# The last FFN pair multiplied with tokens on partitions, fused with the transposes of the final norm

## The chip, the cores and the metric

The kernel runs on one core of one Trainium2 chip. The metric is the device time of one execution in microseconds (us). Engines are called by the profile's names: PE (TensorE matmul), PEld (its weight load), DVE (VectorE), ACT (ScalarE), POOL (GpSimd) and SP (SyncE, which here only issues DMAs).

## The reference, cut to what matters

One layer of a streaming encoder over 1024 prompt and 64 sample tokens, with 1024 features. What counts here is its end: the second half-step feed-forward network (FFN, 2816 hidden features) and the final RMSNorm.

```python
def _rmsnorm(x, g):
    y = x * lax.rsqrt(jnp.mean(x * x, axis=-1, keepdims=True) + EPS)
    return y * g

def _swiglu_half(x, g, w_gate, w_up, w_down):
    h = _rmsnorm(x, g)
    return 0.5 * ((jax.nn.silu(h @ w_gate) * (h @ w_up)) @ w_down)

x = x + _swiglu_half(x, g_ffn2, w2_gate, w2_up, w2_down)    # (1088, 1024)
y = _rmsnorm(x, g_final)                                    # the first two outputs
```

## The kernel before, in words

All 1088 tokens (T) stay on the chip as X, features on partitions: eight tiles (KT) of 128 features by 1088 tokens. The tokens are cut into three tiles NTILE of 364, 362 and 362. Each engine has its own instruction stream, written out by hand; the streams meet in semaphores only, and each executes its instructions in the order of the code.

The down projection of an FFN runs over 11 pairs of 128-feature groups of the hidden layer (p = 0 to 10, LAST = 10). For each pair, SP loads the two activation tiles (AR) and the two weight tiles (RAWD). ACT rounds them to fp32r as the high parts (`down_high`, L1144 and L1147), POOL and DVE subtract to get the low parts (`down_a_low`, L1159, and `down_low`, L1154). Buffers alternate: AB and WB of index 2 (ABe, WBe in the trace) hold the even pairs and so the last one. PE then runs `pe_down`: for each of 3 token tiles and 8 feature tiles a chain of six matmuls (two groups, each as hi·hi, hi·lo and lo·hi in `three_pass`, L248 to L250), with the weights stationary and 362 or 364 tokens moving, into one of six banks in turn (DOWN_BANK). DVE adds half of each chain's result to X (`dve_x`, L1194). That is 24 chains and 24 adds for a pair.

After the last pair PE waits for all adds, and transposes X to tokens on partitions, in nine blocks of 128 tokens (the last has 64): two banks of 512 features for each, four transposes to a bank (L2468), with four blocks of banks in turn. For each block ACT squares and sums each bank (L1850), DVE adds the two sums (L2174), ACT takes the root (L1852), DVE the reciprocal (L2176), and DVE multiplies by it and by the gain GF while it copies the two banks to YO (L2182). SP stores the block (L1401, and L1403 for the sample block). PE takes block b's banks again when YO of block b-4 is written. POOL loads GF, the gain broadcast to all partitions, behind the last chain of the last pair (L1600), because GF lies on the bytes of WBe; DVE waits for that load before its first step of the norm.

Of the kernel before, what the change touches and what calls it, by code (L numbers as in the profile page):

```python
# [13 lines left out]
F32 = mybir.dt.float32  # L14
F32R = mybir.dt.float32r
ACT = mybir.ActivationFunctionType
ALU = mybir.AluOpType
AX = mybir.AxisListType

P = 128  # L20
D = 1024
KT = D // P
SEQ, DEC = 1024, 64
T = SEQ + DEC
NB = SEQ // P
# [30 lines left out]
def build(nc, a, o):  # L56

    with ExitStack() as ctx:
# [4 lines left out]
        def place(name, shape, dtype, offset):  # L63
            return nc.alloc_sbuf_tensor_at(name, shape, dtype, offset=base + offset)
# [14 lines left out]
        rWG = region("wg", 2 * 4 * 4096)  # L79
        rRAW = region("raw", 4 * 4096)  # L80
        rD = region("d", 3 * 8192)
# [4 lines left out]
        X = place("X", [P, KT, T], F32, rX)  # L86
# [27 lines left out]
        AB = [place("AB0", [P, 2, 2, T], F32R, rHL), place("ABo", [P, 2, 2, T], F32R, rHL + 4 * T * 4), place("ABe", [P, 2, 2, T], F32R, rA)]  # L114
        WB = [place("WB0", [P, 2, 2, D], F32R, rWG), place("WBo", [P, 2, 2, D], F32R, rWG + 16384), place("WBe", [P, 2, 2, D], F32R, rD)]
        AR0 = place("AR0", [P, 2, T], F32, rD + 26112)
        AR = [[place(f"AR{f}{i}", [P, 2, T], F32, (rX, rHH)[f] + (2 - i) % 2 * 2 * T * 4) for i in range(2)] for f in range(2)]
        RAWD = [place("RAWDe", [P, 2, D], F32, rRAW), place("RAWDo", [P, 2, D], F32, rRAW + 8192)]
# [38 lines left out]
        assert 4096 + LH * (LD + 4) * 4 <= 7552 and 9600 + 2048 <= 8 * NW * 4  # L157

        YO = place("YO", [P, 4, D], F32, rHH)
        GF = place("GF", [P, D], F32, rD)  # L160
        JUNK = place("JUNK", [P, 4, 512], F32, rT)


# [54 lines left out]
        def named(prefix, names):  # L218
            return namedtuple(prefix, names)(*[sem(f"{prefix}_{n}") for n in names.split()])
# [16 lines left out]
        mo_in = sem("mo_in")  # L236
        m_ = named("m", "d qw ex kt vt gt kw v ot s asm num cn w dn sq norm v2 rs rc sc yt y hi lo cs cout")
        att_hi, att_lo, o_add = sem("att_hi"), sem("att_lo"), sem("o_add")
        fin = named("fin", "sum y")
        fin_out = [sem(f"fin_out{i}") for i in range(4)]  # L240

        def x_view(k, n):
# [883 lines left out]
                    pe_stage(pe, f, p, i // 2, i % 2)  # L1126


        def a_raw(f, odd, start):
            return AR0 if start else AR[f][odd]  # L1130

        def down_high(act, f, p, odd, i, what, start=False):
            which = 0 if start else 2 - odd
            if start:
                act.wait_ge(s_.mm, 280 * f + 28 * LAST - 7 + (1 if what == "a" else i + 1))
            elif what == "a" or odd:
                act.wait_ge(s_.dmm, p * 24 + (264 * f - 24))
            else:
                act.wait_ge(s_.dmm, p * 24 + (264 * f - 24))
            half = (p - odd) * 8 if not isinstance(p, int) else (p - odd) // 2 * 16  # L1140
            loads = half + ((80 if odd else 96) * f + 16)
            if what == "a":
                act.wait_ge(s_.a_in1 if odd else s_.a_in0, loads)
                nc.scalar.activation(AB[which][:, 0, i], a_raw(f, odd, start)[:, i], ACT.Copy).then_inc(s_.ahi, 1)  # L1144
            else:
                act.wait_ge(s_.d_in1 if odd else s_.d_in0, loads)
                nc.scalar.activation(WB[which][:, 0, i], RAWD[odd][:, i], ACT.Copy).then_inc(s_.dhi, 1)  # L1147

        def down_low(dve, f, p, odd, i, start=False):
            which = 0 if start else 2 - odd  # L1150
            dve.wait_ge(s_.dhi, p * 2 + (22 * f + i + 1))
            if start:
                dve.wait_ge(s_.mm, 280 * f + 28 * LAST - 7 + 2 + i + 1)
            nc.vector.tensor_tensor(WB[which][:, 1, i], RAWD[odd][:, i], WB[which][:, 0, i].bitcast(F32), ALU.subtract).then_inc(s_.dlo, 1)  # L1154

        def down_a_low(engine, tensor_tensor, f, p, odd, i, start=False):
            which = 0 if start else 2 - odd
# [1 line left out]
            tensor_tensor(AB[which][:, 1, i], a_raw(f, odd, start)[:, i], AB[which][:, 0, i].bitcast(F32), ALU.subtract).then_inc(s_.alo, 1)  # L1159

        DOWN_BANK = (0, 1, 2, 3, 6, 7)

        def pe_down(pe, f, p, odd, n, start=False, between=None, at=None):
            t0, w = NTILE[n]
            which = 0 if start else 2 - odd
            if n == 0:
                pe.wait_ge(s_.alo, p * 2 + (22 * f + 2))
                pe.wait_ge(s_.dlo, p * 2 + (22 * f + 2))
                if start:
                    pe.wait_ge(s_.ev, 200 * f + 197)  # L1170
                    pe.wait_ge(s_.cp, 80 * f + 80)
            for m in range(KT):
                i = 8 * n + m
                if start and i == 4:
                    pe.wait_ge(s_.ev, 200 * f + 200)
                if not (start and i < 6):
                    pe.wait_ge(s_.xadd, p * 24 + (264 * f + i - 5))
                c = slice(m * P, m * P + P)
                for d in range(2):
                    mm = three_pass(BANK[DOWN_BANK[i % 6]], w, WB[which][:, 0, d, c], WB[which][:, 1, d, c],  # L1180
                                    AB[which][:, 0, d, t0:t0 + w], AB[which][:, 1, d, t0:t0 + w], d == 0, d == 1)
                mm.then_inc(s_.dmm, 1)
                if m == at:
                    between()

        def dve_x(dve, f, p, n, tiles=range(KT), start=False):
            t0, w = NTILE[n]
            if start:
                dve.wait_ge(x_in[n], 16 * f + 32)
            for m in tiles:  # L1190
                i = 8 * n + m
                x = (X2, X)[f][:, m, t0:t0 + w]
                dve.wait_ge(s_.dmm, p * 24 + (264 * f + i + 1))
                nc.vector.scalar_tensor_tensor(out=x, in0=BANK[DOWN_BANK[i % 6]][:, 0:w], scalar=0.5, in1=x,  # L1194
                                               op0=ALU.mult, op1=ALU.add).then_inc(s_.xadd, 1)
# [116 lines left out]
        def _(sp):  # L1312
# [82 lines left out]
            ffn_sp(sp, 1, a["w2_gate"][0], a["w2_up"][0], a["w2_down"][0])  # L1395


            for b in range(NB + 1):
                sp.wait_ge(fin.y, 2 * b + 2)
                if b < NB:  # L1400
                    sp.dma_start(o[0][0, b * P:(b + 1) * P, :], YO[:, b % 4, :]).then_inc(fin_out[b % 4], 16)  # L1401
                else:
                    sp.dma_start(o[1][0, :, :], YO[0:DEC, b % 4, :]).then_inc(fin_out[b % 4], 16)  # L1403
            for i in range(4):
                sp.wait_ge(fin_out[i], 16 * ((NB - i) // 4 + 1))

        @block.gpsimd
        def _(pool):
# [187 lines left out]

            up_pool(pool, 1)
            down_pool(pool, 1)
            pool.wait_ge(s_.dmm, 2 * 264)
            pool.dma_start(GF[:, :], a["g_final"][0].partition_broadcast(P)).then_inc(const_in, 16)  # L1600

        @block.scalar
        def _(act):
# [242 lines left out]
            for b in range(NB + 1):  # L1846
                L = P if b < NB else DEC
                for half in range(2):
                    act.wait_ge(x_tr, 18 + 2 * b + half + 1)
                    nc.scalar.activation(JUNK[0:L, (2 * b + half) % 4, :], BANK[(2 * b + half) % 8][0:L, :], ACT.Square, accum_out=FS[0:L, b % 4, half:half + 1]).then_inc(st.sq, 1)  # L1850
                act.wait_ge(fin.sum, b + 1)
                nc.scalar.activation(FS[0:L, b % 4, 2:3], FS[0:L, b % 4, 2:3], ACT.Sqrt, bias=EPSC[0:L, 0:1], scale=1.0 / D).then_inc(st.rs, 1)  # L1852

        @block.vector
        def _(dve):
# [306 lines left out]
            start_dve_pair(dve, 1)  # L2162
            up_dve(dve, 1)
            down_dve(dve, 1)
            for n in range(3):
                dve_x(dve, 1, LAST, n)


            dve.wait_ge(const_in, 16 * 12)
            for b in range(NB + 1):  # L2170
                L = P if b < NB else DEC
                f = FS[0:L, b % 4]
                dve.wait_ge(st.sq, 23 + 2 * b + 2)
                nc.vector.tensor_tensor(f[:, 2:3], f[:, 0:1], f[:, 1:2], ALU.add).then_inc(fin.sum, 1)  # L2174
                dve.wait_ge(st.rs, 11 + b + 1)
                nc.vector.reciprocal(f[:, 3:4], f[:, 2:3]).then_inc(st.rc, 1)  # L2176
                dve.wait_ge(st.rc, 11 + b + 1)
                if b >= 4:
                    dve.wait_ge(fin_out[b % 4], 16 * (b // 4))
                for half in range(2):  # L2180
                    c = slice(512 * half, 512 * half + 512)
                    nc.vector.scalar_tensor_tensor(out=YO[0:L, b % 4, c], in0=BANK[(2 * b + half) % 8][0:L, :], scalar=f[:, 3:4], in1=GF[0:L, c],  # L2182
                                                   op0=ALU.mult, op1=ALU.mult).then_inc(fin.y, 1)

        @block.tensor
        def _(pe):
# [267 lines left out]
            start_pe_pair(pe, 1)  # L2454
            up_pe(pe, 1)
            down_pe(pe, 1)
            for n in range(3):
                pe_down(pe, 1, LAST, 0, n)


            pe.wait_ge(s_.xadd, 2 * 264)
            for b in range(NB + 1):
                L = P if b < NB else DEC
                if b >= 4:
                    pe.wait_ge(fin.y, 2 * (b - 3))
                for half in range(2):
                    for k in range(4):
                        tr = nc.tensor.transpose(BANK[(2 * b + half) % 8][0:L, k * P:(k + 1) * P], X[:, 4 * half + k, b * P:b * P + L], IDENT[:, :])  # L2468
                    tr.then_inc(x_tr, 1)


# [26 lines left out]
```

## Time and profile before

| | us |
|---|---|
| median of 3 runs (2073.39, 2077.08, 2077.32) | 2077.08 |
| the profiled execution | 2074.57 |
| its span | 2072.7 |
| PE busy in the span | 2028.5 |
| DVE busy | 1169.3 |
| granted PE clock, mean (1.00 is full) | 0.991 |

The span reaches from the first instruction of the profiled execution to the last; the device time of the same execution is 1.87 us longer. Start times in the rows count from the start of the span. PE and PEld overlap. A matmul's duration covers its whole way through the array, so that back-to-back matmuls overlap in the timeline and their pace is the distance of their starts. A row with a count (x32) merges instructions that follow each other and gives the time from the first start to the last end. PEclk is the granted share of TensorE's full clock of 2.4 GHz: 1.00 is 2.4 GHz, 0.50 is 1.2 GHz, and values between are means over both. In the rows of stretches DMA is the mean busy share of the 16 DMA engines. `bank` is any of the eight banks of the accumulator memory.

### The profile page before, as it was taken

What the parts mean: (1) busy time and instruction counts of PE and PEld (TensorE: products, weight loads), DVE (VectorE), ACT (ScalarE), POOL (GpSimd) and SP (SyncE); (2) the same over time, 40 slices, a digit from 0 to 9 for tenths busy, and PEclk for the clock granted to TensorE, in tenths of its full rate; (3) what the DMA queues carried; (4) which work ended last, traced back from release to release, by engine and by line L of the source; (5) the groups of instructions that cost most, each with busy time, mean ns of one, the idle gap of its engine ahead of it and who ended that gap; (6) DMA issues with size and microseconds to landing.
All of it is one profiled execution on the core that took longest, in us unless ns stands there. A gap on an engine that the chain in (4) does not pass through costs nothing.

```text
span 2072.7 us, 38383 instructions
## 1 busy us (share of the span) xinstructions
PE 2028.5 (98%) x14285; PEld 1982.6 (96%) x14285; DVE 1169.3 (56%) x2016; ACT 691.9 (33%) x1371; POOL 711.9 (34%) x732
## 2 busy tenths in 40 slices
PE   7999999999999999999999889999999999999997
PEld 7999999999999999899988889999999999999996
DVE  6755445545666676754446554674444544666665
ACT  6333333333112134633335432343333333311112
POOL 2255555563112200322122530046555555421110
PEclk9999999999999999999999999999999999999998
DMA  7122212226322120333232623212212222622202
GB/s 254 43 85 72 93 62 75 80 79 231 121 84 83 43 73 28 108 98 99 86 97 88 189 67 106 74 63 77 79 62 83 72 93 83 233 99 101 93 0 97
DMA packets 151957, 194.62 MB, mean 94 GB/s; under 512 B 11449, under 2 KB 117465, under 8 KB 151873
## 3 DMA queue, kind: packets, MB, share of 16 engines
q1 hardware_dynamic: 144176, 173.85, 25.5%
q0 software_dynamic: 7696, 19.63, 3.0%
q8 instruction: 55, 0.90, 0.2%
q14 instruction: 30, 0.24, 0.0%
HBM read 142.43 MB, written 50.96 MB: 93 GB/s over the span
## 4 chain that ended last, share of the span: by engine, by line
PE 91%; DVE 3%; issue 3%; ACT 2%; DMA 1%; POOL 0%; SPq 0%; DVEq 0%; ACTq 0%; POOLq 0%
PE bank L248 29%; PE bank L249 28%; PE bank L250 28%; PE bank L2264 1%; PE bank L2283 1%; PE bank L2274 1%; PE bank L743 1%; PE bank L283 1%; DMA XIN<-in_x_prompt 1%; DVE YO L2182 1%; PE bank L2206 0%; DVE WN L2082 0%; PE bank L2364 0%; PE bank L2372 0%; PE bank L2374 0%
## 5 line engine op out<-in xcount | busy, mean ns | idle before, releaser
L1194 DVE SCALAR_TENSOR_TENSOR X<-bank,X 128x362 f32<-128x362 f32 (+1 forms) x528 | 275.1, 533 | 192.6 <-PE bank L250 192.6
L248 PE MATMUL bank<-HH,WGH 128*128 128x362 f32 (+2 forms) x808 | 264.5, 327 | 1.5 <-DVE X L2095 1.5
L250 PE MATMUL bank<-HH,WGL 128*128 128x362 f32 (+2 forms) x808 | 255.3, 316 | 0.0
L249 PE MATMUL bank<-HL,WGH 128*128 128x362 f32 (+2 forms) x808 | 255.2, 316 | 0.0
L248 PE MATMUL bank<-FC,WR 128*128 128x272 f32 x768 | 223.0, 290 | 1.0 <-issue 0.7
L250 PE MATMUL bank<-FC,WR 128*128 128x272 f32 x768 | 222.3, 289 | 0.0
L249 PE MATMUL bank<-FC,WR 128*128 128x272 f32 x768 | 221.5, 288 | 0.0
L589 DVE TENSOR_TENSOR PV<-bank,PV 128x272 f32<-128x272 f32 x280 | 122.6, 439 | 147.9 <-PE bank L250 107.7
L656 POOL TENSOR_TENSOR SA<-SA,PV 128x272 f32<-128x272 f32 x160 | 136.2, 871 | 112.9 <-DVE PV L589 109.8
L248 PEld LDWEIGHTS bank<-HH,WGH 128*128 128x128 f32 x808 | 153.1, 189 | 16.7 <-issue 13.9
L469 DVE TENSOR_TENSOR WR<-RAWU,WR 128x512 fp32r<-128x512 f32 x100 | 86.4, 864 | 131.5 <-ACT WR L464 131.5
L248 PE MATMUL bank<-ABe,WBe 128*128 128x362 f32 (+1 forms) x480 | 158.5, 330 | 0.0
L248 PE MATMUL bank<-ABo,WBo 128*128 128x362 f32 (+1 forms) x480 | 158.1, 329 | 0.0
L249 PE MATMUL bank<-ABo,WBo 128*128 128x362 f32 (+1 forms) x480 | 157.7, 329 | 0.0
L249 PE MATMUL bank<-ABe,WBe 128*128 128x362 f32 (+1 forms) x480 | 157.6, 328 | 0.0
L250 PE MATMUL bank<-ABo,WBo 128*128 128x362 f32 (+1 forms) x480 | 156.7, 326 | 0.0
L250 PE MATMUL bank<-ABe,WBe 128*128 128x362 f32 (+1 forms) x480 | 156.6, 326 | 0.0
L249 PEld LDWEIGHTS bank<-HL,WGH 128*128 128x128 f32 x808 | 152.9, 189 | 1.6
L250 PEld LDWEIGHTS bank<-HH,WGL 128*128 128x128 f32 x808 | 152.7, 189 | 0.0
L248 PEld LDWEIGHTS bank<-FC,WR 128*128 128x128 f32 x768 | 144.8, 189 | 2.0 <-issue 1.1
L249 PEld LDWEIGHTS bank<-FC,WR 128*128 128x128 f32 x768 | 145.2, 189 | 0.0
L250 PEld LDWEIGHTS bank<-FC,WR 128*128 128x128 f32 x768 | 145.2, 189 | 0.0
(350 smaller groups left out, 5577.7 us busy)
## 6 DMA issues: line engine op xcount, KB each, us to landing
asp<-SA SPq DMA_DIRECT2D x44, 544.0 KB, 3.1
AR<-asp SPq DMA_DIRECT2D x22, 1088.0 KB, 5.0
RAWG<-in_w_gate SPq DMA_DIRECT2D x22, 1024.0 KB, 5.9
RAWU<-in_w_up SPq DMA_DIRECT2D x22, 1024.0 KB, 5.2
RAWDe<-in_w_down SPq DMA_DIRECT2D x12, 1024.0 KB, 4.9
RAW<-in_w_in SPq DMA_DIRECT2D x22, 512.0 KB, 3.7
RAWDo<-in_w_down SPq DMA_DIRECT2D x10, 1024.0 KB, 5.0
xsp<-X SPq DMA_DIRECT2D x8, 1088.0 KB, 6.9
```

The costliest lines, as they stand in the source:

```text
L248: nc.tensor.matmul(bank[:, 0:w], w_hi, rhs_hi, start=first, stop=False)
L249: nc.tensor.matmul(bank[:, 0:w], w_hi, rhs_lo, start=False, stop=False)
L250: return nc.tensor.matmul(bank[:, 0:w], w_lo, rhs_hi, start=False, stop=last)
L283: mm = nc.tensor.matmul(BANK[NORM_BANK[n]][:, 0:w], ONES[:, :], SQH[:, k, t0:t0 + w], start=(k == 0), stop=(k == KT - 1))
L469: nc.vector.tensor_tensor(WR[:, o, 1], weight(o, q0, mat), WR[:, o, 0].bitcast(F32), ALU.subtract).then_inc(s_.lo, 1)
L589: nc.vector.tensor_tensor(out, bank, add, ALU.add).then_inc(s_.ev, 1)
L656: nc.gpsimd.tensor_tensor(gated(j, slot), gated(j, slot), PV[j][:, tile], ALU.mult).then_inc(s_.mul, 1)
L743: mm = nc.tensor.matmul(BANK[4 + n][:, 0:HT], ONES[:, :], SQT[:, kh, k], start=(kh == 0 and k == 0), stop=(kh == 1 and k == 3))
L1194: nc.vector.scalar_tensor_tensor(out=x, in0=BANK[DOWN_BANK[i % 6]][:, 0:w], scalar=0.5, in1=x, op0=ALU.mult, op1=ALU.add).then_inc(s_.xadd, 1)
L2182: nc.vector.scalar_tensor_tensor(out=YO[0:L, b % 4, c], in0=BANK[(2 * b + half) % 8][0:L, :], scalar=f[:, 3:4], in1=GF[0:L, c], op0=ALU.mu ...
L2264: mm = nc.tensor.matmul(BANK[2 + i // 2][:, (i % 2) * 256:(i % 2) * 256 + 256], QB[rows, par, 2 * g_ + hl // 2, :], KW[rows, par, 0 if g_ ...
L2274: tr = nc.tensor.transpose(BANK[4 + w][:, i * P:(i + 1) * P], SP[:, i, w * P:(w + 1) * P], IDENT[:, :])
```

## The change

For the last pair of the second FFN the roles are turned: the activations (128 hidden features by 128 tokens) are stationary, and the down weights move, 512 features wide. Each half block starts its bank with four transposes of X (which by then holds everything but this pair), and adds six matmuls onto them, so that the bank holds the final x with tokens on partitions. The half of the half-step is put into the weights (`scale=0.5` in ACT's copy, a multiplication in DVE's subtraction). The 24 chains, the 24 adds of DVE and the separate transposes of the last pair are gone. The norm takes its blocks from `token_bank`, where the banks come in another turn. GF moves to bytes that are free after pair 0, and its load waits only for pair 1; it stands in POOL's stream behind POOL's last subtraction. The sample block is stored in two halves.

```diff
-        GF = place("GF", [P, D], F32, rD)
+        GF = place("GF", [P, D], F32, rWG)
...
+        def by_token(f, p):
+            return f == 1 and isinstance(p, int) and p == LAST
...
-                nc.scalar.activation(WB[which][:, 0, i], RAWD[odd][:, i], ACT.Copy).then_inc(s_.dhi, 1)
+                nc.scalar.activation(WB[which][:, 0, i], RAWD[odd][:, i], ACT.Copy, scale=0.5 if by_token(f, p) else 1.0).then_inc(s_.dhi, 1)
...
-            nc.vector.tensor_tensor(WB[which][:, 1, i], RAWD[odd][:, i], WB[which][:, 0, i].bitcast(F32), ALU.subtract).then_inc(s_.dlo, 1)
+            if by_token(f, p):
+                nc.vector.scalar_tensor_tensor(out=WB[which][:, 1, i], in0=RAWD[odd][:, i], scalar=0.5, in1=WB[which][:, 0, i].bitcast(F32),
+                                               op0=ALU.mult, op1=ALU.subtract).then_inc(s_.dlo, 1)
+            else:
+                nc.vector.tensor_tensor(WB[which][:, 1, i], RAWD[odd][:, i], WB[which][:, 0, i].bitcast(F32), ALU.subtract).then_inc(s_.dlo, 1)
...
+        TOKEN_BANK = (4, 0, 2, 6)
+
+        def token_bank(b, half):
+            return BANK[TOKEN_BANK[b % 4] + half]
+
+        def pe_token_block(pe, b):
+            L, t0 = (P if b < NB else DEC), b * P
+            done = 264 + LAST * 24
+            if b == 0:
+                pe.wait_ge(s_.alo, LAST * 2 + (22 + 2))
+                pe.wait_ge(s_.dlo, LAST * 2 + (22 + 2))
+            if b < 4:
+                pe.wait_ge(s_.xadd, done - 24 + (8, 20, 22, 24)[b])
+            else:
+                pe.wait_ge(fin.y, 2 * (b - 3))
+            for half in range(2):
+                bank, c = token_bank(b, half), slice(512 * half, 512 * half + 512)
+                for k in range(4):
+                    nc.tensor.matmul(bank[0:L, k * P:(k + 1) * P], X[:, 4 * half + k, t0:t0 + L], IDENT[:, :], is_transpose=True, start=k == 0, stop=False)
+                for d in range(2):
+                    a_hi, a_lo = (AB[2][:, i, d, t0:t0 + L] for i in range(2))
+                    w_hi, w_lo = (WB[2][:, i, d, c] for i in range(2))
+                    nc.tensor.matmul(bank[0:L, :], a_hi, w_hi, start=False, stop=False)
+                    nc.tensor.matmul(bank[0:L, :], a_hi, w_lo, start=False, stop=False)
+                    mm = nc.tensor.matmul(bank[0:L, :], a_lo, w_hi, start=False, stop=d == 1)
+                mm.then_inc(fin.mm, 1)
...
 # SP
-                    sp.dma_start(o[1][0, :, :], YO[0:DEC, b % 4, :]).then_inc(fin_out[b % 4], 16)
+            for half in range(2):
+                c = slice(512 * half, 512 * half + 512)
+                sp.wait_ge(fin.y, 2 * NB + half + 1)
+                sp.dma_start(o[1][0, :, c], YO[0:DEC, NB % 4, c]).then_inc(fin_out[NB % 4], 16)
...
 # POOL
-            pool.wait_ge(s_.dmm, 2 * 264)
+            pool.wait_ge(s_.dmm, 264 + 48)
...
 # ACT
-                    act.wait_ge(x_tr, 18 + 2 * b + half + 1)
-                    nc.scalar.activation(JUNK[0:L, (2 * b + half) % 4, :], BANK[(2 * b + half) % 8][0:L, :], ACT.Square, accum_out=FS[0:L, b % 4, half:half + 1]).then_inc(st.sq, 1)
+                    act.wait_ge(fin.mm, 2 * b + half + 1)
+                    nc.scalar.activation(JUNK[0:L, (2 * b + half) % 4, :], token_bank(b, half)[0:L, :], ACT.Square, accum_out=FS[0:L, b % 4, half:half + 1]).then_inc(st.sq, 1)
...
 # DVE
-            for n in range(3):
-                dve_x(dve, 1, LAST, n)
...
-                    nc.vector.scalar_tensor_tensor(out=YO[0:L, b % 4, c], in0=BANK[(2 * b + half) % 8][0:L, :], scalar=f[:, 3:4], in1=GF[0:L, c],
+                    nc.vector.scalar_tensor_tensor(out=YO[0:L, b % 4, c], in0=token_bank(b, half)[0:L, :], scalar=f[:, 3:4], in1=GF[0:L, c],
...
 # PE
-            for n in range(3):
-                pe_down(pe, 1, LAST, 0, n)
-            pe.wait_ge(s_.xadd, 2 * 264)
...
+            for b in range(NB + 1):
+                pe_token_block(pe, b)
```

## Rows read from the trace of the kernel before

**Rows 1.** The page's first part: busy us, share of span, instructions by engine.

```profile
PE 2028.5 (98%) x14285; PEld 1982.6 (96%) x14285; DVE 1169.3 (56%) x2016; ACT 691.9 (33%) x1371; POOL 711.9 (34%) x732
```

**Rows 2.** The page's fourth part: shares of the chain that ended last.

```profile
PE 91%; DVE 3%; issue 3%; ACT 2%; DMA 1%; POOL 0%; SPq 0%; DVEq 0%; ACTq 0%; POOLq 0%
```

**Rows 3.** Stretches: start:end, length, busy of PE, PEld, DVE, ACT, POOL, PEclk, DMA, GB/s.

```profile
2022.72:2046.62 23.90, 23.90 (x145) 23.75 (x144) 12.85 (x24) 0.00 (x0) 0.00 (x0) 1.00 0.00 1
2046.62:2072.70 26.08, 10.65 (x73) 8.88 (x72) 15.35 (x37) 14.41 (x46) 0.59 (x1) 0.79 0.51 192
```

**Rows 4.** Chain of waits in time, last stretch: start us, us, what.

```profile
2047.08 3.90 DMA GF<-in_g_final
```

**Rows 5.** Timeline of PE, last pair on: start us, us, instruction, [idle before].

```profile
2022.72 0.33 PE L248 MATMUL bank<-ABe,WBe 128*128 128x364 f32 x1
2046.45 0.33 PE L250 MATMUL bank<-ABe,WBe 128*128 128x362 f32 x1
2047.40 3.71 PE L2468 MATMUL bank<-IDENT,X 128*128 128x128 f32 x32 [0.63 <-DVE X L1194]
```

**Rows 6.** Timeline of PE, matmuls of 272 and 364 columns.

```profile
499.84 0.29 PE L248 MATMUL bank<-FC,WR 128*128 128x272 f32 x1
502.12 0.33 PE L248 MATMUL bank<-AB,WB 128*128 128x364 f32 x1
503.95 0.33 PE L250 MATMUL bank<-AB,WB 128*128 128x364 f32 x1
```

**Rows 7.** Timeline of PE, transposes behind and between fp32r matmuls.

```profile
874.59 0.32 PE L250 MATMUL bank<-HH,WGL 128*128 128x362 f32 x1
874.84 1.74 PE L2214 MATMUL bank<-IDENT,R 4*128 4x4 f32 x27
...
1233.50 0.29 PE L250 MATMUL bank<-HH,WGL 128*128 128x272 f32 x1
1233.62 0.60 PE L2385 MATMUL bank<-IDENT,WN 128*128 128x128 f32 x4
1234.18 0.29 PE L249 MATMUL bank<-HL,WGH 128*128 128x272 f32 x1
```

**Rows 8.** Timeline of ACT, table load and last square of the norm.

```profile
2049.38 1.28 ACT L1852 ACT_TABLE_LOAD   x1
...
2066.22 0.58 ACT L1850 ACTIVATE JUNK<-bank 64x512 f32<-64x512 f32 x1
2066.69 0.19 ACT L1850 ACTIVATION_READ_ACCUMULATOR JUNK<-bank 64x1 f32 x1
```

**Rows 9.** Timeline of DVE: last weights, two x adds, last block's norm.

```profile
2007.47 2.35 DVE L1154 TENSOR_TENSOR WBe<-RAWDe,WBe 128x1024 fp32r<-128x1024 f32 x2
...
2022.91 0.53 DVE L1194 SCALAR_TENSOR_TENSOR X<-bank,X 128x362 f32<-128x362 f32 x1 [0.47 <-PE bank L250]
...
2046.81 0.54 DVE L1194 SCALAR_TENSOR_TENSOR X<-bank,X 128x362 f32<-128x362 f32 x1 [0.46 <-PE bank L250]
...
2067.30 0.14 DVE L2174 TENSOR_TENSOR FS<-FS 64x1 f32<-64x1 f32 x1
...
2067.99 1.40 DVE L2182 SCALAR_TENSOR_TENSOR YO<-bank,FS,GF 64x512 f32<-64x512 f32 x2
```

**Rows 10.** Timeline of the SP queue, the last store.

```profile
2069.41 0.55 SPq L1403 DMA_DIRECT2D out<-YO  x1
```

**Rows 11.** DMA issues, last stretch: count, KB each, median us to landing.

```profile
out<-YO SPq DMA_DIRECT2D x8, 512.0 KB, 2.6
out<-YO SPq DMA_DIRECT2D x1, 256.0 KB, 2.9
```

**Rows 12.** Stretches as above: transposes among matmuls, and after idle time.

```profile
1220.00:1240.00 20.00, 18.52 (x138) 16.38 (x137) 10.64 (x33) 5.79 (x20) 5.61 (x6) 1.00 0.01 1
2055.00:2057.00 2.00, 1.78 (x8) 1.57 (x8) 1.60 (x5) 1.45 (x5) 0.00 (x0) 0.50 0.62 252
```

**Rows 13.** DVE groups by form: count | busy us, mean ns.

```profile
L296 DVE SCALAR_TENSOR_TENSOR SQa<-X,GC,SQH 128x362 f32<-128x362 f32 x8 | 4.2, 592 | 0.1
```

More of the change, by code:

```diff
@@ L238, in build @@
         att_hi, att_lo, o_add = sem("att_hi"), sem("att_lo"), sem("o_add")
-        fin = named("fin", "sum y")
+        fin = named("fin", "mm sum y")
         fin_out = [sem(f"fin_out{i}") for i in range(4)]
@@ L1395, in _ @@
             ffn_sp(sp, 1, a["w2_gate"][0], a["w2_up"][0], a["w2_down"][0])
-            for b in range(NB + 1):
+            for b in range(NB):
                 sp.wait_ge(fin.y, 2 * b + 2)
-                if b < NB:
-                    sp.dma_start(o[0][0, b * P:(b + 1) * P, :], YO[:, b % 4, :]).then_inc(fin_out[b % 4], 16)
-                else:
-                    sp.dma_start(o[1][0, :, :], YO[0:DEC, b % 4, :]).then_inc(fin_out[b % 4], 16)
+                sp.dma_start(o[0][0, b * P:(b + 1) * P, :], YO[:, b % 4, :]).then_inc(fin_out[b % 4], 16)
+            for half in range(2):
+                c = slice(512 * half, 512 * half + 512)
+                sp.wait_ge(fin.y, 2 * NB + half + 1)
+                sp.dma_start(o[1][0, :, c], YO[0:DEC, NB % 4, c]).then_inc(fin_out[NB % 4], 16)
             for i in range(4):
-                sp.wait_ge(fin_out[i], 16 * ((NB - i) // 4 + 1))
+                sp.wait_ge(fin_out[i], 16 * ((NB - i) // 4 + 1 + (i == NB % 4)))
         @block.gpsimd
@@ L2456, in _ @@
             down_pe(pe, 1)
-            for n in range(3):
-                pe_down(pe, 1, LAST, 0, n)
-            pe.wait_ge(s_.xadd, 2 * 264)
             for b in range(NB + 1):
[L2463 to L2469, printed above, removed]
+                pe_token_block(pe, b)
 _INS = ["x_prompt", "x_sample", "cache_k", "cache_v", "state_C", "state_n", "state_m", "g_ffn1", "w1_gate", "w1_up", "w1_down",
```

## Prediction, on record before the result was known

> **What bounds the kernel now.** I read the page's first part and then its chain: PE is busy 98% of the span [rows 1] and makes up 91% of the chain that ended last [rows 2]. Everywhere but at the end, then, only PE's own work counts. The change touches the end alone, so I cut the span there. PE starts the last pair of the second FFN at 2022.72 and its last matmul of it at 2046.45 [rows 5]. Up to 2046.62 PE is busy without a hole, at the full granted clock [rows 3]; from there to the end at 2072.70 lie 26.08 us in which PE is busy for 10.65 and in which DVE, ACT and the stores take turns [rows 3]. So the last 50 us have two halves: 23.9 us bounded by PE, and a tail of 26.1 us that a chain of small steps bounds, behind a load of GF of 3.90 us [rows 4].
>
> **The change on PE.** Removed are 24 chains of six matmuls, 144 in 23.90 us, 0.166 us each [rows 3]. Added are 9 blocks x 2 halves x 6 = 108 matmuls with 512 columns, and the 72 transposes, which were there before but lay in the tail. No row has 512 columns in fp32r; the pace of fewer columns gives it. With 272 columns 18 starts lie in 502.12 - 499.84 = 2.28 us, 0.1267 each; with 364 columns 11 lie in 503.95 - 502.12 = 1.83 us, 0.1664 each [rows 6]. The slope is 0.0397 / 92 = 0.43 ns for a column, and 148 more columns make 0.230. From below, neither width runs quicker than its columns at 2.4 GHz (113 and 152 ns), which makes 0.213; from above, in proportion to 364 columns, 0.234. At 2.4 GHz for each added column it is 0.228. I take 0.229, between that and the slope.
>
> The Trainium skill has a figure here: "TensorE: Matmul & The Clock Gate", "Wait — 56ns, not 53.3ns?", says that warm matmuls start every N/2.4 GHz plus about 2.5 ns, some 216 ns at 512 columns. The trace has 15 ns over the pure columns at both widths [rows 6], not 2.5, so I stay with the rows; by the page the 108 matmuls would be 108 x 13 ns = 1.4 us quicker, as an estimate.
>
> A transpose of 128x128 among fp32r matmuls: from the start at 1233.50 to that at 1234.18 lie two matmuls of 272 columns and four transposes, so (0.68 - 2 x 0.127) / 4 = 0.107 us each, the two changes of kind included [rows 7]. In the tail 32 of them take 3.71 us, (3.71 - 0.27) / 31 = 0.111 with 0.27 for the last one's passage [rows 5]. I take 0.110. From above: behind a matmul at 874.59 the transposes start after 0.25 us instead of 0.165 [rows 7], which is 0.085 for a change of kind; 0.107 with none is the lower end.
>
> A block is 12 x 0.229 + 8 x 0.110 = 2.75 + 0.88 = 3.63 us, and nine are 32.7 us. The sample block saves nothing: its 64 tokens are on the stationary side. Bounds: 12 x 0.213 + 8 x 0.107 = 3.41, and 12 x 0.234 + 8 x 0.111 + 2 x 0.085 = 3.87; over nine blocks -2.0 and +2.2 us. PE's stream now ends at 2022.72 + 32.7 = 2055.4, 8.8 us later than before. No weight load stands in the way: PE loaded for each matmul before too, and at the shorter pace of 0.127 as well.
>
> **Does PE run through?** Block 0 wants 8 adds of pair 9, and the low parts of pair 10; DVE wrote the weights' low parts from 2007.47 to 2009.82 [rows 9]. Blocks 1 to 3 want up to all 24 adds; the last starts at 2022.91 and takes 0.53 [rows 9], block 1 is reached at 2026.4. Block 4, reached at 2037.2, wants YO of block 0. That comes at about 2022.72 + 3.63 + 0.16 (passage), then 0.7 for square and sum, 1.28 for the table load [rows 8], 2.1 for sum, root, reciprocal and YO [rows 9]: 2030.6. There are 6.6 us to spare. One block's steps done strictly one after the other are 0.58 + 0.58 + 0.19 + 2.09 = 3.4 us [rows 8, 9], below the 3.63 of PE, so ACT, DVE and with them the banks keep up. A store lands 2.6 us after its issue [rows 11], also inside a block, and YO has four buffers.
>
> **What goes from the tail.** The wait for the last add and the transposes before the norm, the table load and GF's 3.90 us [rows 4] now lie beside PE's stream. GF is issued right behind POOL's last subtraction. PE started the last pair at 2022.72 behind one of pair 9 without a hole [rows 3, 5], so POOL's part was done by then, and with 3.9 us GF lands by 2026.6 at the latest, before the first norm wants it at some 2028.5. Eight of the nine norms lie beside PE too. Dropping 24 adds of 0.54 us on DVE gives nothing by itself, since PE did not wait for them. What remains behind PE's last matmul is the last half block:
> - start of the last matmul: 2055.4 - 0.23 = 2055.15; its passage is its pace plus 0.16 (0.33 against 0.166, [rows 5]): ends at 2055.54;
> - ACT starts the square some 0.05 later (DVE started 0.03 behind PE, [rows 5, 9]); square and read of the sum last from 2066.22 to 2066.88, 0.66 [rows 8]: 2056.25;
> - sum, root, reciprocal and both halves of YO: from 2067.30 to 2067.99 + 1.40, 2.09 [rows 9]: 2058.36;
> - issue 0.02 behind, landing 2.6 to 2.9 [rows 11], I take 2.75; before, the end of the span lay 0.39 behind the landing (2069.41 + 2.9 against 2072.70, [rows 10, 11]): 2061.5.
> The tail becomes 6.1 us. Its first half is issued 0.7 us earlier on SP, which needs 0.55 for an issue [rows 10]: no wait. The smaller transfer may land a few tenths sooner; no row prices it.
>
> **Smaller edits.** ACT's scale is a parameter of the same copy: nothing. DVE's two subtractions become a scalar_tensor_tensor; the nearest row from the same memory takes 592 ns for 362 elements [rows 13], in proportion 1.67 us for 1024 against 1.2: at most 1 us, in front of 13 us of slack (2009.8 to 2022.7). Without that cover it would cost that 1 us.
>
> **Sum.** PE's stream +8.8, tail 6.1 instead of 26.1, -20.0: -11.2 us. The profiled execution would come to 2074.57 - 11.2 = 2063.4. The median shown is 2.5 us above that execution; from it the sum gives 2065.9. The four executions of before lie at 2073.4, 2074.6, 2077.1 and 2077.3, and I start from the middle of median and profiled one, 2075.8: 2064.6.
>
> **Rivals.**
> 1. *Changes of kind are dear.* 36 times PE goes between fp32 transposes and fp32r matmuls that add to the same bank. If each costs the 0.085 us of the one row [rows 7], 3.1 us go: gain 8.1, time 2067.7. Against it: the four transposes at 1233.62 show none. Chance 9%.
> 2. *The clock falls (slower).* A quarter of PE's time in the new stretch is transposes. Where the tail's transposes run after idle time the granted clock is 0.50, 1.2 GHz [rows 12]. At 1.2 GHz a block is 12 x 0.427 + 8 x 0.22 = 6.9 us, 3.3 more. From 3.4 such blocks of nine on the gain is eaten; half the stretch would give 2064.6 + 15 = 2079.5. Against it: from 1220 to 1240 transposes lie among matmuls, PE even idles 1.5 us, and the clock stays at 1.00 [rows 12]; before the half clock PE had been idle for most of the time. Chance 4%.
> 3. *PE waits for banks.* Only if a block's norm took over 3.63 us serially, or block 0's YO came 6.6 us late. A serial chain with 1 us more for each block would be 4.4 against 3.63: 5 blocks x 0.8 = 4 us, time 2068.6. Chance 3%.
>
> On the second the Trainium skill speaks against the change: "TensorE: Matmul & The Clock Gate", "Part 4: PE-mode transpose", says that transposes don't count as activity that releases the full clock. The rows with mixed work agree with it only as far as transposes after idle time go; three quarters of the stretch are matmuls.
>
> That the change does not do what it says concerns the sums in the banks and not the instructions, and so no time.
>
> **How the numbers follow.** The forecast holds 83%, with its own range from 2060.2 (2073.4 - 13.2, where the lower bounds of PE's paces meet the fastest run) to 2068.3 (2077.3 - 9.0). Rivals 9, 4 and 3%, and 1% for something at 2074 or above. The range over all is 2060.0 to 2070.5, and leaves out the slow clock. A measurement here tells some 0.2%, 4 us, from no change. All of the forecast and the first and third rival are faster by more than that, unless two unlikely ends meet: faster 0.94, within 0.2% 0.02, slower 0.04.
>
> **What would show it.** In the changed trace: starts of matmuls 0.229 us apart with 512 columns (over 0.234 or under 0.213 refutes the pace); 3.63 us from block to block, the same for all nine; no hole of PE from 2022.7 to 2055.4; a granted clock of 1.00 there (0.50 is rival 2); GF landed before the first YO; the table load beside PE; idle ACT and DVE waiting for PE in every block (else rival 3); 6.1 us from the end of PE's stream (the last matmul's start plus its pace) to the end of the span. Wrong would be a gain under 9.0 or over 13.2 us at equal base.

## The result, and the profile after

The changed kernel takes 2064.63 us (median of 5 runs, 2059.71 to 2065.51) against 2076.4 us (median of 5, 2073.39 to 2077.32): 0.9942 of the time, with a 95% interval from 0.9927 to 0.9956. That is 12 us by the ratio (9 to 15). The profiled execution took 2065.51 us. A later comparison of the same two gave 0.9948 (0.9934 to 0.9961).

The page of the changed kernel, its first part and the shares of its chain (rows 1 and 2 of before):

```profile
span 2063.7 us, 38288 instructions
...
PE 2027.2 (98%) x14249; PEld 1976.6 (96%) x14249; DVE 1156.7 (56%) x1992; ACT 693.5 (34%) x1371; POOL 712.6 (35%) x732
...
PE 94%; ACT 2%; DVE 2%; DMA 1%; issue 1%; SPq 0%; POOL 0%; DVEq 0%; ACTq 0%
```

PE is still the bound, and its share of the chain rose from 91% to 94%: part of what other engines held at the end is now PE's. The end is best read by itself, from PE's first instruction of the last pair, at 2024.99 now, to the end of the span. Two stretches, in the columns of [rows 3]:

```profile
2024.99:2057.95 32.96, 32.96 (x181) 26.62 (x179) 14.40 (x33) 15.22 (x43) 0.00 (x0) 1.00 0.28 112
2057.95:2063.70 5.75, 0.17 (x1) 0.00 (x0) 1.71 (x4) 0.98 (x3) 0.00 (x0) 0.70 0.42 137
```

32.96 us in which PE never pauses, at a granted clock of 1.00, and a tail of 5.75 us. With 38.71 us this end is 11.27 us shorter than the 49.98 us of before [rows 3]. The span is shorter by only 9.0: PE reaches the last pair 2.27 us later in this execution, with the same work up to there. Over all runs of this study that point lies between 2020.3 and 2027.3 us, so that a span or a time says nothing of tenths here. The end does: in a second profile of the changed kernel it was 38.72 us. From here on "the end" is this length, and the experiments are compared by it.

PE's timeline, two half blocks and the last matmul (answering to [rows 5 to 7]):

```profile
2024.99 0.60 PE L1189 MATMUL bank<-IDENT,X 128*128 128x128 f32 x4
2025.35 0.49 PE L1193 MATMUL bank<-WBe,ABe 128*128 128x512 f32 x1
2025.67 0.39 PE L1194 MATMUL bank<-WBe,ABe 128*128 128x512 f32 x1
...
2026.60 0.40 PE L1195 MATMUL bank<-WBe,ABe 128*128 128x512 f32 x1
2026.84 0.60 PE L1189 MATMUL bank<-IDENT,X 128*128 128x128 f32 x4
...
2054.32 0.60 PE L1189 MATMUL bank<-IDENT,X 128*64 128x128 f32 x4
...
2057.72 0.40 PE L1195 MATMUL bank<-WBe,ABe 128*64 128x512 f32 x1
```

Four transposes start at 2024.99 and six wide matmuls at 2025.35; a half block takes 2026.84 - 2024.99 = 1.85 us, and eight blocks 2054.32 - 2024.99 = 29.33, 3.67 each. The matmul behind the transposes is followed after 0.32, the others after 0.23. The last block, in all engines' order of time (answering to [rows 8 to 10]):

```profile
2058.15 0.59 ACT L1886 ACTIVATE JUNK<-bank 64x512 f32<-64x512 f32 x1 [1.14 <-PE bank L1195]
2058.65 0.19 ACT L1886 ACTIVATION_READ_ACCUMULATOR JUNK<-bank 64x1 f32 x1
2058.87 0.15 DVE L2206 TENSOR_TENSOR FS<-FS 64x1 f32<-64x1 f32 x1 [1.51 <-ACT JUNK L1886]
...
2059.57 1.40 DVE L2214 SCALAR_TENSOR_TENSOR YO<-bank,FS,GF 64x512 f32<-64x512 f32 x2
2060.34 1.18 SPq L1439 DMA_DIRECT2D out<-YO  x2
```

From the start of the last matmul to that of the square are 0.43 us, 0.72 on to the sum, 2.10 to the end of YO, and then a store. The stores (answering to [rows 11]):

```profile
out<-YO SPq DMA_DIRECT2D x8, 512.0 KB, 2.6
out<-YO SPq DMA_DIRECT2D x2, 128.0 KB, 2.3
```

And the three covers: ACT's table load, DVE's first sum and first YO, and POOL's load of GF.

```profile
2029.58 1.28 ACT L1888 ACT_TABLE_LOAD   x1
```

```profile
2029.66 0.16 DVE L2206 TENSOR_TENSOR FS<-FS 128x1 f32<-128x1 f32 x1 [3.93 <-ACT JUNK L1886]
...
2031.40 1.41 DVE L2214 SCALAR_TENSOR_TENSOR YO<-bank,FS,GF 128x512 f32<-128x512 f32 x2
```

```profile
2007.46 0.59 POOL L1636 DMA_DIRECT2D GF<-in_g_final  x1
```

```profile
GF<-in_g_final POOLq DMA_DIRECT2D x1, 512.0 KB, 3.9
```

GF lands at 2011.4 (3.9 us behind its issue, as before), 18 us ahead of DVE's first sum at 2029.66, which waits for ACT and not for GF. The longest waits of the end show who bounds it (waiting line, releaser, us in total, times, longest):

```profile
ACT JUNK L1886 <- PE bank L1195: 36.0, 17, 21.7
DVE FS L2206 <- ACT JUNK L1886: 15.1, 9, 3.9
```

ACT waits for PE at every half block, DVE for ACT at every block; PE is not in the list.

### The profile page after: what moved, and what is told of

The parts are those of the page before. It is cut to its first block, busy times and chain, and to the rows that moved or that the text cites. A ratio compares the mean times of both kernels' runs of the same rounds, so it can differ in the third digit from the quotient of the medians.

```text
span 2063.7 us, 38288 instructions
## 1 busy us (share of the span) xinstructions
PE 2027.2 (98%) x14249; PEld 1976.6 (96%) x14249; DVE 1156.7 (56%) x1992; ACT 693.5 (34%) x1371; POOL 712.6 (35%) x732
## 4 chain that ended last, share of the span: by engine, by line
PE 94%; ACT 2%; DVE 2%; DMA 1%; issue 1%; SPq 0%; POOL 0%; DVEq 0%; ACTq 0%
PE bank L248 29%; PE bank L250 28%; PE bank L249 28%; PE bank L2296 1%; PE bank L2315 1%; PE bank L2306 1%; PE bank L743 1%; PE bank L283 1%; DMA XIN<-in_x_prompt 1%; PE bank L2238 0%; PE bank L1195 0%; PE bank L1193 0%; PE bank L1194 0%; PE bank L2396 0%; PE bank L1189 0%
## 5 line engine op out<-in xcount | busy, mean ns | idle before, releaser
L1229 DVE SCALAR_TENSOR_TENSOR X<-bank,X 128x362 f32<-128x362 f32 (+1 forms) x504 | 262.4, 533 | 180.0 <-PE bank L250 180.0
L515 ACT ACTIVATE SA<-SA 128x272 f32<-128x272 f32 x160 | 66.9, 429 | 227.7 <-DVE SA L589 118.5
L248 PE MATMUL bank<-ABe,WBe 128*128 128x362 f32 (+1 forms) x432 | 142.3, 329 | 0.0
L250 PE MATMUL bank<-ABe,WBe 128*128 128x362 f32 (+1 forms) x432 | 141.4, 327 | 0.0
```

Of the source, the lines that this page charges most:

```text
L248: nc.tensor.matmul(bank[:, 0:w], w_hi, rhs_hi, start=first, stop=False)
L250: return nc.tensor.matmul(bank[:, 0:w], w_lo, rhs_hi, start=False, stop=last)
L515: nc.scalar.activation(tile, tile, ACT.Silu).then_inc(s_.silu, 1)
```

## The experiments

Where no time is given below, the kernel ran once, under the profiler, and its end alone is compared. Each end comes from one profile; where a kernel was profiled twice the two ends differ by 0.01 us (the changed kernel) and 0.04 us (the grouped one).

**GF early alone.** The kernel before, with only GF's place and load changed.

```diff
-        GF = place("GF", [P, D], F32, rD)
+        GF = place("GF", [P, D], F32, rWG)
-            pool.wait_ge(s_.dmm, 2 * 264)
+            pool.wait_ge(s_.dmm, 264 + 48)
```

> The kernel before with one part of the change alone: GF on the bytes of pair 0, loaded behind POOL's last subtraction. I compare the stretch from the first matmul of the last pair to the end of the span: 49.98 us before, 38.71 after the whole change. My theory: the 3.90 us of GF's load lay beside ACT's table load, which ends at 2050.66 where GF landed at 2050.97, so only 0.5 us go: 49.5. Rival: the wait of 3.65 us on GF is worth its length: 46.3.

The end as one stretch, ACT's timeline, and the wait of DVE in the kernel before that the early load was to remove:

```profile
2023.97:2073.30 49.33, 34.50 (x218) 32.59 (x216) 28.20 (x61) 14.41 (x46) 0.00 (x0) 0.89 0.24 91
```

```profile
2050.49 1.28 ACT L1852 ACT_TABLE_LOAD   x1
2051.78 0.30 ACT L1852 ACTIVATE FS<-FS,EPSC 128x1 f32<-128x1 f32 x1
```

```profile
2051.00 0.16 DVE L2174 TENSOR_TENSOR FS<-FS 128x1 f32<-128x1 f32 x1 [3.65 <-DMA GF<-in_g_final]
```

49.33, 0.65 us less; time 0.999 (0.998 to 1.000) of before. DVE had waited 3.65 us for GF, but the first root now stands right behind the table load. A wait is worth only what it lasts beyond the next one.

**The old product, with the norm between its chains.** GF early and the sample block's store in halves are in it too.

```diff
+        TOKEN_BANK = (4, 4, 4, 4, 0, 2, 6, 4, 0)
+        TURN = {9: 0, 13: 1, 17: 2, 20: 3}
+        NORM = {11: 0, 15: 1, 19: 2, 23: 3}
...
+            for i in range(24):
...
+                if i in TURN:
+                    turn_block(pe, TURN[i])
...
+            for i in range(24):
+                dve_x(dve, 1, LAST, i // 8, (i % 8,))
+                if i in NORM:
+                    norm_block(NORM[i])
```

> The last pair multiplied as in the kernel before (weights stationary, 362 to 364 tokens moving, 24 adds on DVE), but the transposes and the norm of token blocks 0 to 3 placed between its chains; GF early and the sample block stored in halves, as in the change. It separates the overlap from the new product. My theory: the gain is the overlap, and the new product only allows more of it. 23.9 us of chains + 4 blocks x 0.88 of transposes = 27.4, then the last add 0.6, norm 3 and five norms of 2.03 on DVE, 12.7 from the last add, and 2.7 for the store: 43 us (42 to 44.5) against 49.98 and 38.71. Rival: the wide product itself brings the gain, and this stays at 48 or more.

The end, and what PE waited for:

```profile
2026.43:2073.40 46.97, 32.78 (x217) 31.19 (x216) 27.75 (x61) 14.88 (x46) 0.00 (x0) 0.93 0.25 96
```

```profile
PE bank L1178 <- DVE YO L2214: 3.9, 4, 1.8
```

46.97, time 0.9975 (0.9961 to 0.9990): neither number. PE stood 3.9 us in front of transposes, because DVE had not yet written the YO whose banks they wanted. Three of the four waits, 3.3 us together, lie in front of the transposes of blocks 1 to 3, between the chains; the fourth, 0.56, lies behind them, in front of the last block. The 3.3 us are most of the 4.0 by which I missed, and they came of my placing: so the same once more, placed otherwise (the wait for GF moves with the first norm). (The expectation of the second version calls all 3.9 us waits between the chains.)

```diff
-        TURN = {9: 0, 13: 1, 17: 2, 20: 3}
-        NORM = {11: 0, 15: 1, 19: 2, 23: 3}
+        TURN = {8: 0, 13: 1, 17: 2, 21: 3}
+        NORM = {10: 0, 14: 1, 18: 2, 23: 3}
```

> The product of before with transposes and norms of blocks 0 to 3 between its chains, the transposes now behind chains 8, 13, 17 and 21, the norms behind adds 10, 14, 18 and 23. The first version's stretch was 46.97, with 3.9 us of PE waiting for YO between the chains. My theory: PE has no such wait now, its chains end at 27.5 us from the start, and the rest stays 15.8: 43.3. Rival: the waits only move to other places, 46 or more.

```profile
2022.61:2066.00 43.39, 32.42 (x218) 31.18 (x216) 27.37 (x61) 14.86 (x46) 0.00 (x0) 0.91 0.27 103
```

```profile
2050.11 0.32 PE L250 MATMUL bank<-ABe,WBe 128*128 128x362 f32 x1
2051.06 3.72 PE L1178 MATMUL bank<-IDENT,X 128*128 128x128 f32 x32 [0.63 <-DVE X L1230]
```

```profile
2050.92 0.15 DVE L2206 TENSOR_TENSOR FS<-FS 128x1 f32<-128x1 f32 x1
```

43.39. The last chain's last matmul starts 2050.11 - 2022.61 = 27.50 us from the start, with only 0.15 us of waiting ahead of it. Behind it DVE still has the norms of six blocks: block 3's begins at 2050.92, the five others follow, 2.03 us each. So of the 11.27 us GF's early load is 0.65; the transposes of four blocks and the norms of three laid beside the old product are 5.94 (some 0.6 of it the store in halves, by what a run below shows for the changed kernel); and the new product is 4.68.

The new product finishes tokens block by block, and only one norm is left behind it instead of six. PE has done with it after 32.96 us, against 27.7 for the last chain here; but here the transposes of five blocks are still to come, 40 x 0.109 = 4.4 us, so that PE's whole work differs by less than 1 us. Two things stay open. The new product also takes the 24 adds off DVE, and no run separates that from the order of the tokens. And 4.68 is what it adds to this placing: block 4 (tokens 512 to 639) lies in the second token tile as well, its x is complete after 16 chains, and yet its transposes wait here for the last add. How much of the 4.68 us a better placing of the old product would win is not shown.

**Fewer changes between transposes and matmuls.** The eight transposes of a block together, then its twelve matmuls.

```diff
             for half in range(2):
-                bank, c = token_bank(b, half), slice(512 * half, 512 * half + 512)
+                bank = token_bank(b, half)
                 for k in range(4):
                     nc.tensor.matmul(bank[0:L, k * P:(k + 1) * P], X[:, 4 * half + k, t0:t0 + L], IDENT[:, :], is_transpose=True, start=k == 0, stop=False)
+            for half in range(2):
+                bank, c = token_bank(b, half), slice(512 * half, 512 * half + 512)
```

> The changed kernel, with the eight transposes of a block's two banks in front of its twelve matmuls: 18 changes of kind instead of 36. My theory: a change of kind costs nothing that can be seen, the stretch stays at 38.7 (38.5 to 38.9). Rival 1 of the prediction: each costs up to 0.085 us, and 1.5 us go: 37.2.

The end was 38.30; time 0.9931 (0.9906 to 0.9957). The 362-column matmuls ahead of it ran faster in that execution (163.5 against 166.7 ns), and I took the 0.4 us for that. Both kernels again, side by side on one chip:

> The changed kernel once more, on the same chip as the next one. My theory: 5.5 to 6 thousandths faster than before again; the stretch from the first instruction of the last pair to the end of the span is 38.7 us where the 362-column matmuls ahead of it run at 166.7 ns, and some 0.5 us less where they run at 163.5 (the paces seen so far in one and the same code). Rival: the stretch is 38.7 whatever that pace is.

> The kernel with a block's eight transposes in front of its twelve matmuls, beside the changed kernel on one chip. Its stretch was 38.30 against 38.71, but its matmuls of 362 columns ahead of the stretch ran at 163.5 ns against 166.7. My theory: the 0.4 us are that pace and not the grouping; time the same as the changed kernel within the interval, and the sum of a block over 12 matmul paces 0.88 us in both. Rival: the changes of kind cost 0.4 us or more, and this kernel is again the shorter one at equal pace.

The changed kernel's end was 38.72 and this one's 38.26, behind 362-column matmuls at 166.1 and 165.7 ns (means over 14 us). My explanation fell: the end is the same whatever that pace is, and grouping saves 0.43 us. The times do not separate the two kernels (0.9948, 0.9934 to 0.9961; 0.9930, 0.9917 to 0.9944). PE of the grouped kernel (second profile), one block:

```profile
2023.74 1.04 PE L1189 MATMUL bank<-IDENT,X 128*128 128x128 f32 x8
2024.53 0.48 PE L1195 MATMUL bank<-WBe,ABe 128*128 128x512 f32 x1
2024.85 0.40 PE L1196 MATMUL bank<-WBe,ABe 128*128 128x512 f32 x1
...
2025.31 0.39 PE L1195 MATMUL bank<-WBe,ABe 128*128 128x512 f32 x1
...
2027.12 0.39 PE L1197 MATMUL bank<-WBe,ABe 128*128 128x512 f32 x1
2027.36 0.82 PE L1189 MATMUL bank<-IDENT,X 128*128 128x128 f32 x6
```

Eight transposes and the first matmul's longer step take 2024.85 - 2023.74 = 1.11 us. Then ten steps (from one matmul's start to the next) take (2027.12 - 2024.85) / 10 = 0.227 each, where four in the changed kernel take (2026.60 - 2025.67) / 4 = 0.2325 each. By their place in the row, as means over all blocks: in the grouped kernel the second step takes 0.232, the third 0.230, the ones from the fourth to the eleventh 0.226 to 0.228 (in the rows above (2027.12 - 2025.31) / 8 = 0.226), and the last one, in front of the next transposes, 0.232. In the changed kernel the second to the sixth take 0.232, 0.233, 0.233, 0.228 and 0.233.

**No transposes.** The norm here works on the last pair's product alone; x is left out.

```diff
-                for k in range(4):
-                    nc.tensor.matmul(bank[0:L, k * P:(k + 1) * P], X[:, 4 * half + k, t0:t0 + L], IDENT[:, :], is_transpose=True, start=k == 0, stop=False)
-                    nc.tensor.matmul(bank[0:L, :], a_hi, w_hi, start=False, stop=False)
+                    nc.tensor.matmul(bank[0:L, :], a_hi, w_hi, start=d == 0, stop=False)
```

> The changed kernel without the 72 transposes of X (the norm then works on the last pair's product alone, x is left out). My theory: 72 x 0.110 = 7.9 us less: 30.8 for the stretch, a block of 12 x 0.233 = 2.80 us, still above what the norm needs for a block. Rival: the transposes' changes of kind cost more than a run of transposes shows, 9 us or more go; or the norm's serial chain of 3.4 us now holds PE, and the stretch stays above 34.

```profile
2022.68 0.40 PE L1191 MATMUL bank<-WBe,ABe 128*128 128x512 f32 x1
...
2023.61 0.39 PE L1192 MATMUL bank<-WBe,ABe 128*128 128x512 f32 x1
...
2026.33 0.39 PE L1192 MATMUL bank<-WBe,ABe 128*128 128x512 f32 x1
```

The end was 30.32: the 72 transposes cost 8.39 us, not 7.9. The matmuls start with four steps of (2023.61 - 2022.68) / 4 = 0.2325 and go on with twelve of 0.2267. So wide matmuls step slower next to a change of kind, on both sides of it, and with six to a bank most of them stand next to one. That is not the whole of it: the fourth step behind a change takes 0.227 in the grouped kernel and 0.233 in the changed one. The norm kept up although PE now needs only 12 x 0.227 = 2.7 us for a block: the tail was 5.78. The 3.4 us of a block's steps done one after the other, which the prediction compared with PE's block, is more than what a block costs when ACT and DVE work on neighbouring blocks (2.03 us a block in the kernel with norms between the chains).

**Four times the transposes.**

```diff
-                for k in range(4):
-                    nc.tensor.matmul(bank[0:L, k * P:(k + 1) * P], X[:, 4 * half + k, t0:t0 + L], IDENT[:, :], is_transpose=True, start=k == 0, stop=False)
+                for j in range(16):
+                    k = j % 4
+                    nc.tensor.matmul(bank[0:L, k * P:(k + 1) * P], X[:, 4 * half + k, t0:t0 + L], IDENT[:, :], is_transpose=True, start=k == 0, stop=k == 3 and j < 12)
```

> The changed kernel, with each set of four transposes done four times over (the later ones write the same values again): 288 transposes instead of 72, so that transposes are some 56% of PE's time. My theory: 216 more at 0.111 us, all at the full granted clock, +24.0 us: 62.7 for the stretch. Rival (the slow clock): transposes don't hold the clock up, it falls to 1.2 GHz for all or part of the stretch, which makes 70 to 120.

```profile
2022.84:2050.00 27.16, 27.16 (x195) 24.62 (x194) 6.46 (x16) 7.98 (x21) 0.00 (x0) 1.00 0.15 59
2050.00:2079.00 29.00, 29.00 (x203) 25.53 (x202) 7.94 (x18) 7.37 (x22) 0.00 (x0) 1.00 0.22 91
```

The end was 62.26, and the granted clock is 1.00 over these 27 us and over the 29 that follow. 216 more transposes cost 23.55 us, 0.109 each. So of the 8.39 us above, 72 x 0.109 = 7.85 are transposes and 0.54 are left for the 36 changes, 0.015 us each on the mean. With more than half of PE's time in transposes, in sets of 16 with six matmuls behind each, the clock does not fall. The rule of the Trainium skill ("TensorE: Matmul & The Clock Gate", "Part 4: PE-mode transpose") that transposes don't count towards the full clock does not show in such a mix; what a long stretch of transposes alone would do, no run here tells.

**GF late.** The changed kernel, GF's load held back until block 3 is multiplied.

```diff
-            pool.wait_ge(s_.dmm, 264 + 48)
+            pool.wait_ge(fin.mm, 8)
```

> The changed kernel with GF's load held back until four blocks are multiplied, which shows what the cover is worth and what a wait for banks costs (rival 3 of the prediction). My theory: GF is issued 14.9 us into the stretch and lands at 18.8; YO of block 0 comes at 20.9 instead of 7.8, PE waits for it from 14.7 on, 6.2 us, and no block behind it waits again, since DVE takes 2.03 a block and PE 3.67: stretch 44.9, a little more where the granted clock falls behind the idle time. Rival: as in the kernel before only a part shows, because other waits lie beside it: under 42.

PE where it goes on with block 4, and two stretches around and behind that point:

```profile
2047.39 1.11 PE L1189 MATMUL bank<-IDENT,X 128*128 128x128 f32 x4 [6.40 <-DVE YO L2214]
...
2049.16 0.63 PE L1195 MATMUL bank<-WBe,ABe 128*128 128x512 f32 x1
2049.59 0.63 PE L1193 MATMUL bank<-WBe,ABe 128*128 128x512 f32 x1
```

```profile
2042.00:2050.00 8.00, 2.60 (x8) 2.24 (x9) 3.60 (x10) 3.42 (x12) 0.00 (x0) 0.74 0.32 131
2050.00:2060.00 10.00, 10.00 (x50) 8.24 (x49) 6.28 (x14) 5.16 (x17) 0.00 (x0) 0.87 0.52 210
```

47.73, 9.0 more than the changed kernel. PE waited 6.40 us for YO (I had said 6.2) and only once. The other 2.6 us are the clock: behind the idle time PE starts at 1.2 GHz, steps of 0.43 instead of 0.23, and is back at 0.23 some 5 us on. So a cover matters twice on PE, and this is also what rival 2 would have looked like: its 0.427 for a step was right, its cause was idle time and not transposes.

**One store.**

```diff
-            for half in range(2):
-                c = slice(512 * half, 512 * half + 512)
-                sp.wait_ge(fin.y, 2 * NB + half + 1)
-                sp.dma_start(o[1][0, :, c], YO[0:DEC, NB % 4, c]).then_inc(fin_out[NB % 4], 16)
+            sp.wait_ge(fin.y, 2 * NB + 2)
+            sp.dma_start(o[1][0, :, :], YO[0:DEC, NB % 4, :]).then_inc(fin_out[NB % 4], 16)
```

> The changed kernel with the sample block stored in one DMA of 256 KB, as before. The halves landed 2.3 us after their issue, the whole one 2.9, in the kernel before. My theory: most of those 0.6 us were the store of block 7 ahead of it, which is now long gone; the size alone is 0.1 to 0.3 us: stretch 38.8 to 39.0. Rival: the halving is worth all 0.6: 39.3.

```profile
out<-YO SPq DMA_DIRECT2D x1, 256.0 KB, 2.9
```

39.32, 0.61 more, and this store lands after 2.9 us as in the kernel before, though block 7's is long gone: my theory was wrong and the rival right, the halving is worth all 0.6. It is not the number of bytes alone, as the stores of 512 KB, from 128 partitions instead of 64, land after 2.6; what sets the 2.9, no run here separates.

**A shorter tail.** On the grouped kernel: transposes of two blocks together, and the sample block's YO shared by ACT and DVE.

```diff
+                if b == NB:
+                    nc.vector.tensor_tensor(YO[0:L, b % 4, 0:512], token_bank(b, 0)[0:L, :], GF[0:L, 0:512], ALU.mult).then_inc(z.padded, 1)
...
+            act.wait_ge(st.rc, 11 + NB + 1)
+            act.wait_ge(z.padded, 2)
+            nc.scalar.activation(YO[0:DEC, NB % 4, 0:512], YO[0:DEC, NB % 4, 0:512], ACT.Copy, scale=FS[0:DEC, NB % 4, 3:4]).then_inc(dist_abs, 1)
...
+            for blocks in ((0,), (1, 2), (3, 4), (5, 6), (7, 8)):
+                pe_token_blocks(pe, blocks)
```

> Built on the version with grouped transposes (stretch 38.3): the transposes of two blocks stand together (blocks 1 and 2, 3 and 4, 5 and 6, 7 and 8), which leaves 5 groups instead of 9, and in the sample block DVE multiplies the first half by GF while PE works on the second, so that ACT can scale it (some 0.5 us) beside DVE's 0.70 for the second half. My theory: the grouping saved 0.43 us for 9 groups fewer, 4 more give 0.2; the tail's two halves of YO take 0.7 instead of 1.4: stretch 37.4, time 6 to 7.5 thousandths under before. Rival: the paired blocks come so late that the norm of block 7 runs into that of block 8, and the tail gives the gain back: 38.2 or more.

ACT's and DVE's halves of YO, and SP's two issues:

```profile
2054.39 0.72 ACT L1896 ACTIVATE YO<-YO,FS 64x512 f32<-64x512 f32 x1 [0.22 <-DVE FS L2220]
2054.39 0.74 DVE L2226 SCALAR_TENSOR_TENSOR YO<-bank,FS,GF 64x512 f32<-64x512 f32 x1
2055.14 1.18 SPq L1444 DMA_DIRECT2D out<-YO  x2
```

38.21, time 0.9945 (0.9931 to 0.9958). Both halves are ready 2.59 us behind the last matmul's start instead of 3.25, but then SP issues one store behind the other (1.18 us for both), and the end is where it was. Pairing the blocks brought 0.05 us, not 0.2. So ACT issues one of the two stores:

```diff
+            act.wait_ge(dist_abs, 2)
+            act.dma_start(o[1][0, :, 0:512], YO[0:DEC, NB % 4, 0:512]).then_inc(fin_out[NB % 4], 16)
```

> The previous version, in which both halves of the sample block's YO were ready 0.66 us earlier behind the last matmul (2.59 against 3.25), and yet the span ended where it had: SP issued the two stores one behind the other, 0.6 us apart, from the moment both were ready. Here ACT issues the store of the half that it scaled, SP the other. My theory: the two issues run side by side, the tail is 5.1 us instead of 5.75: stretch 37.6. Rival: the end is set by something else behind the stores (two queues that end apart, or the landing of both together takes 2.9 us as one of 256 KB does): 38.2.

```profile
2058.21 0.58 ACTq L1896 DMA_DIRECT2D out<-YO  x1
2058.23 0.55 SPq L1442 DMA_DIRECT2D out<-YO  x1
```

```profile
out<-YO ACTq DMA_DIRECT2D x1, 128.0 KB, 2.3
out<-YO SPq DMA_DIRECT2D x1, 128.0 KB, 2.9
```

38.14, time 0.9941 (0.9927 to 0.9955). Now both are issued at 2058.2, and SP's lands after 2.9 us, as long as one store of 256 KB takes, while ACT's lands after 2.3. The rival holds: the 0.66 us won ahead of the store are given back in it, in the first version to the second issue, in this one to a landing that is 0.6 us longer. That the two transfers hold each other up is the likely reason, but one profile does not show it. Neither version can be told from the grouped one by its time. The grouped kernel is the simplest that is shorter than the changed one at its end (38.28 against 38.72).

## Why the prediction was right

The forecast was 2064.6 us and the measured median 2064.63; the closeness of the times is luck, as they spread by 6 us, and the base of 2075.8 was a choice between executions. The end of the profile is the fair test: 49.98 to 38.71, -11.27, where the sum said -11.2. That these two agree so well is luck too, as the steps show: two misses of a third of a microsecond cancelled. By its steps:

- *Pace of the wide matmuls.* Taken 0.229 from a line through two widths. Measured 0.2267 to 0.2325, and 108 x 0.227 = 24.5 us without transposes (24.7 in the sum). The prediction read 15 ns over the pure columns at both of its widths; at 272 columns the rows give 13 (126.7 - 113.3), and at 512 it became 13 to 19. The 0.216 of "Wait — 56ns, not 53.3ns?" in the Trainium skill's page "TensorE: Matmul & The Clock Gate" would have been 1.2 us too little.
- *Transposes.* 0.110 for each was right (0.109). The changes of kind, taken as nothing beyond it, cost 0.54 us in all, most of it in the steps of the wide matmuls next to them. Together with the first term PE's stream became 32.96 instead of 32.7.
- *PE runs through.* No wait in the list of waits, YO of block 0 at 2032.81, 7.82 us into the stretch; the forecast had 2030.6 - 2022.7 = 7.9. The prediction gave this cover 6.6 us to spare; with GF late it was lost, PE waited 6.40, and the 2.6 us of lost clock behind that were not in my price of rival 3.
- *GF and table load.* Said to go beside PE, and they did. GF's early load alone is worth 0.65 us and not 3.9; the sum never counted it apart, as it set the new tail against the old one. The table load was not tested alone.
- *Smaller edits.* DVE's two subtractions with the 0.5 were given up to 1 us more, under cover. They take 2.35 us in both kernels: the edit costs nothing.
- *Tail.* 6.1 forecast, 5.75 measured. The mis-sized term is the last store: 2.75 taken, 2.3 measured for half the size, which I had called a few tenths that no row prices.
- *Rival 1* (dear changes): there is a price, but 0.015 us and not 0.085 each; 0.54 us, of which 0.43 can be had back. *Rival 2* (clock): refuted with four times the transposes. *Rival 3* (banks): no wait.

The two misses are +0.3 on PE and -0.35 in the tail.

## What to carry to other kernels

When the bound engine stops before the end of a kernel, look at how late the first finished piece of the output comes: a product that finishes tokens block by block may cost PE some more time (here 1 us in 33, its transposes included) and still win, because eight of nine norms and stores hide beside it. Price a removed wait by what ends next behind it, not by its length (3.65 us waited for GF, 0.65 won). On PE price a new long wait with the clock that it loses (6.4 us of idle time cost 9.0); in the first interleaved kernel five waits of 0.6 to 1.8 us lost none, the granted clock was 1.00 until PE had done.

## What the runs showed that I had not expected

- Wide fp32r matmuls step by up to 0.233 us next to a change between transposes and matmuls and at the start of a row behind matmuls of another shape, and by 0.227 away from it, at a granted clock of 1.00 throughout. Without any transpose the sample block, with 64 tokens stationary, steps by 0.230. Why, no run here tells.
- The same 362-column matmuls run at paces between 163.2 and 166.8 ns in different parts of one execution and at the same place in different ones, at the full granted clock (steps averaged over 4 us each). Over the more than 14,000 matmuls of this kernel some ns matter; the point where the last pair starts moved by 7 us between executions. How much of that is this pace is open.
- Of two stores of 128 KB on two queues issued together, one lands after 2.3 us and the other after 2.9, like one of 256 KB (one profile), while on one queue a store that follows the other by 0.66 us lands after 2.3.
